# Two interleaved context lanes, doubled weight buffers and six gather landings in a fused transformer kernel

## The reference, cut to what matters

```python
for l in range(2):                                 # first_block, h is 256 x 1024
    ...                                            # attention, w_o, layer norm
    ffn = peer_ffn(h, peer_wq[l], ...)             # 8 heads x 16 experts for each token:
    #   sc = q . sub_keys; top-k twice -> eidx (256 tokens x 128 rows), g = softmax
    #   a = gelu(u[eidx] . h);  ffn = sum over 128 of (g * a) * v[eidx]
    h = layer_norm(ALPHA * h + ffn, ln2_g[l], ln2_b[l])
# second_block
sh1, sc1, g1, sh2, sc2, g2 = split(silu(c) @ w_mod + b_mod, 6)      # modulation
hc = rmsnorm(ctx) * (1 + cm[1]) + cm[0]
sf_c = state_features(hc, ...)                     # Rk, Rv, Gk, Gv, gates (conv for Gk, Gv)
init = recurrent_mixers(sf_c, None, None, zeros)   # retention and gated delta rule states,
#   forward and backward, two chunks of 128 tokens each; depends on ctx alone, not on x
...                                                # the same for x with init, then 64 experts
```

## Time and profile before

| | |
|---|---|
| median of 3 runs | 3200.03 us (3195.45 to 3200.51) |
| the profiled execution | 3195.45 us, span 3193.5 us |
| PE busy | 2481.0 us (78%) |
| DVE busy | 1622.7 us (51%) |
| ACT, POOL busy | 836.7, 824.5 us (26% each) |
| moved by DMA | 885.92 MB, mean 277 GB/s |

### The profile page before, as it was taken

The page is one execution under the profiler, slowest core; times in us unless marked ns, Lnnn a source line. Parts: engine busy times, 40 slices in busy tenths (PEclk is TensorE's granted clock), DMA queues, the critical chain, the costliest instruction groups (busy, mean ns, idle before and its releaser), DMA issues.

```text
span 3193.5 us, 29065 instructions
## 1 busy us (share of the span) xinstructions
PE 2481.0 (78%) x9500; PEld 1316.5 (41%) x9500; DVE 1622.7 (51%) x3307; ACT 836.7 (26%) x2262; POOL 824.5 (26%) x717
## 2 busy tenths in 40 slices
PE   6688888897899868998877877768777667676673
PEld 3665334353455466633322222546553433222221
DVE  4535536879877653664758544264523422111112
ACT  1212333443444131233333333322110111011110
POOL 1001323354465100233344433012000013122221
PEclk9689999999999968999999999889888779888896
DMA  6026978898999702699999999310113199999992
GB/s 258 1 80 264 367 294 337 356 374 326 400 382 391 282 23 80 271 422 422 422 421 417 421 421 386 132 40 27 53 53 148 40 381 400 394 382 389 381 379 80
DMA packets 128898, 885.92 MB, mean 277 GB/s; under 512 B 23008, under 2 KB 23392, under 8 KB 31584
## 3 DMA queue, kind: packets, MB, share of 16 engines
q0 software_dynamic: 86976, 553.74, 43.2%
q1 hardware_dynamic: 41760, 330.22, 25.6%
HBM read 877.56 MB, written 37.75 MB: 287 GB/s over the span
## 4 chain that ended last, share of the span: by engine, by line
PE 42%; DMA 26%; DVE 20%; ACT 5%; issue 4%; POOL 1%; SPq 1%; DVEq 0%; POOLq 0%; ACTq 0%
PE ps L155 41%; DMA ring<-in_peer_uv,idx_u 10%; DVE ring L1256 6%; DMA ring<-in_w_gu 5%; DVE arena L76 5%; ACT arena L125 3%; DMA ring<-in_w_down 3%; DMA arena<-in_w_gu 2%; PE ps L158 2%; DVE arena L97 2%; DMA ring<-in_w_mod 1%; DMA ring<-in_w_in 1%; SPq L2479 1%; DVE iu L113 1%; POOL small L134 1%
## 5 line engine op out<-in xcount | busy, mean ns | idle before, releaser
L155 PE MATMUL ps<-ring,arena 128*128 128x512 f32 (+3 forms) x3264 | 1270.2, 649 | 308.6 <-ACT arena L125 180.8
L155 PEld LDWEIGHTS ps<-ring,arena 128*128 128x128 f32 (+2 forms) x3264 | 472.6, 180 | 988.6 <-issue 606.5
L1256 DVE CUSTOM_DVE_ANT_0 ring<-ring,h 128x1024 f32<-128x1024 f32 x448 | 566.1, 1264 | 331.5 <-DMA ring<-in_peer_uv,idx_u 294.8
L2297 POOL DMA_INDIRECT ring<-in_peer_uv,idx_u x448 | 489.7, 1093 | 811.3 <-PE ps L155 672.9
L155 PE MATMUL ps<-arena 128*128 128x128 f32 (+7 forms) x2504 | 509.8, 389 | 156.6 <-DVE arena L97 45.9
L125 ACT ACTIVATE arena<-arena 128x1 f32<-128x1 f32 (+4 forms) x1129 | 312.9, 277 | 742.4 <-DVE arena L1256 650.5
L155 PEld LDWEIGHTS ps<-arena 128*128 128x128 f32 (+3 forms) x2504 | 328.8, 199 | 332.1 <-issue 158.9
L155 PE MATMUL ps<-ring,hT 128*128 128x512 f32 (+1 forms) x704 | 325.8, 619 | 44.5 <-DMA ring<-in_w_in 22.6
L76 DVE TENSOR_TENSOR arena<-arena,ps 128x512 f32<-128x512 f32 (+1 forms) x158 | 93.6, 592 | 465.2 <-ACT arena L125 356.5
L125 ACT ACTIVATE arena<-ps 128x512 f32<-128x512 f32 (+4 forms) x180 | 99.0, 550 | 834.6 <-PE ps L155 762.8
L125 ACT ACTIVATE arena<-cst,arena 128x128 f32<-128x128 f32 x512 | 205.5, 401 | 155.6 <-PE ps L155 114.2
(11 more groups left out here) (115 smaller groups left out, 1481.9 us busy)
## 6 DMA issues: line engine op xcount, KB each, us to landing
ring<-in_w_gu SPq DMA_DIRECT2D x98, 1024.0 KB, 29.0
ring<-in_w_down SPq DMA_DIRECT2D x52, 1024.0 KB, 29.1
ring<-in_w_in SPq DMA_DIRECT2D x22, 2048.0 KB, 9.8
arena<-in_w_gu SPq DMA_DIRECT2D x30, 1024.0 KB, 29.5
ring<-in_w_mod SPq DMA_DIRECT2D x12, 2048.0 KB
ring<-in_peer_wq SPq DMA_DIRECT2D x8, 2048.0 KB, 7.9
ring<-in_w_o SPq DMA_DIRECT2D x6, 2048.0 KB, 11.6
arena<-in_w_down SPq DMA_DIRECT2D x12, 1024.0 KB, 25.4
```

The costliest lines, as they stand in the source:

```text
L155: return self.e.matmul(o, lhsT, rhs, start=start, stop=stop, skip_group_check=True)
L1256: v.done(v.e.tensor_tensor_reduce(out=row, in0=row, in1=h[:, n // 128, :], scale=1.0, scalar=0.0, op0=ALU.mult, op1=ALU.add, accum_out=aa[ ...
L2297: g.e.indirect_dma_start(out=landing(n), out_offset=None, in_=d["peer_uv"], in_offset=bass.IndirectOffsetOnAxis(ap=idx_u[:, n:n + 1], axis ...
```

## The change

It does five things.

1. GATHERS goes from 8 to 6. The landings in ring 0 to 3 fall away; gathers 4 and 5 wait for the keys, and gather n is issued when gather n - 6 is used.
2. Background weight blocks alternate between ring 0 to 3 (even) and ring 16 to 19 (odd). SP issues block i when block i - 2 is used; the first waits for wq 3, the second for wq 2.
3. The two directions of the context's states, lanes with storage of their own (in the ring's two places and the arena), run side by side, step by step (together), and take PSUM banks from 4 to 7 and 0, 1 (LATE).
4. Modulation takes one step for each block. With the lanes side by side the background of layer 0 has 80 steps: 6, 14, 17, 5 and 38. They stand at n = 4, 7, ... 127 and 138, 141, ... 249. So the states take the 38 steps from 138 on. Layer 1 has 10 steps at n = 4, 14, ... 94.
5. The first w_in block and the second w_o block of layer 1 wait for the lanes' last use. Block Rk of x goes into ring 0 to 3 after modulation block 10, during layer 1's gathers.

```diff
-GATHERS = 8
-SUMS, OTHERS = ((0, 1), (2, 3)), (4, 5, 6, 7)
+GATHERS = 6
+SUMS, OTHERS, LATE = ((0, 1), (2, 3)), (4, 5, 6, 7), (4, 5, 6, 7, 0, 1)
...
     if l:
-        return 1 if n in range(4, 94, 5) else 0
-    return 1 if n in range(2, 130, 2) or n in range(138, 254, 2) else 0
+        return 1 if n in range(4, 104, 10) else 0
+    return 1 if n in range(4, 130, 3) or n in range(138, 252, 3) else 0
...
-        ctx_tiles = [ar(14720 + 512 * i, 512) for i in range(11)] + [ar(512 * i, 512) for i in (1, 2)]
-        ctx_kd = ar(1536, 512)
+        ctx_tiles = [R(i, 1)[:, 512 * j:512 * j + 512] for i in (0, 1, 2, 3, 16, 17, 18, 19) for j in range(2)]
+        ctx_tiles += [ar(14720 + 512 * i, 512) for i in range(9)] + [ar(19328, 512), ar(19840, 512), ar(0, 512)]
+        ctx_lanes = [(ctx_tiles[0:13], ctx_tiles[26]), (ctx_tiles[13:26], ctx_tiles[27])]
...
-            return R(4 + 2 * i, 2) if i < 5 else ar(6144, 2048) if i == 5 else R(2 * i - 12, 2)
+            return R(4 + 2 * i, 2) if i < 5 else ar(6144, 2048)
...
         def BG(i):
-            return R(16, 4)
+            return R(0 if i % 2 == 0 else 16, 4)
...
                 def lane(dr):
+                    TT, kd = ctx_lanes[dr]
                     for c in ((0, 1) if dr == 0 else (1, 0)):
-                        yield from gdn_chunk(s, dr, c, ctx_tiles, OTHERS)
-                        yield from ret_chunk(s, dr, c, ctx_kd, None, OTHERS)
-
-                return chain(lane(0), lane(1))
+                        yield from gdn_chunk(s, dr, c, TT, LATE)
+                        yield from ret_chunk(s, dr, c, kd, None, LATE)
+
+                return together(lane(0), lane(1))
...
-                return chain(lane(0), lane(1))
+                yield from together(lane(0), lane(1))
+                v.tell(("used", "ctx lanes"))
...
             def modulate(blocks, before):
                 for i in blocks:
-                    block(16, 4, d["w_mod"][i], ("loaded", "w_mod", i),
-                          after=[("used", "w_mod", i - 1) if i > blocks[0] else before])
+                    block(0 if i % 2 == 0 else 16, 4, d["w_mod"][i], ("loaded", "w_mod", i),
+                          after=[("used", "w_mod", i - 2) if i - blocks[0] > 1 else before[i % 2]])
...
-                block(0, 4, d["w_in"][l, 0], ("loaded", "w_in", l, 0), after=last)
+                block(0, 4, d["w_in"][l, 0], ("loaded", "w_in", l, 0), after=[("used", "ctx lanes")] if l else ())
...
-                      after=[("used", "ctx", "Gv")] if l else [("used", "ln0")])
+                      after=[("used", "ctx lanes")] if l else [("used", "ln0")])
...
-                before = ("used", "wq", l, 2)
+                before = [("used", "wq", l, 3), ("used", "wq", l, 2)]
...
-                    ctx_block(0, "Rk", ("used", "w_mod", 3))
-                    ctx_block(1, "Rv", ("used", "ctx", "Rk"))
-                    ctx_block(2, "Gk", ("used", "ctx", "Rv"))
-                    ctx_block(3, "Gv", ("used", "ctx", "Gk"))
+                    ctx_block(0, "Rk", ("used", "w_mod", 2))
+                    ctx_block(1, "Rv", ("used", "w_mod", 3))
+                    ctx_block(2, "Gk", ("used", "ctx", "Rk"))
+                    ctx_block(3, "Gv", ("used", "ctx", "Rv"))
...
+            block(0, 4, d["w_in2"][0], ("loaded", "x", "Rk"), after=[("used", "w_mod", 10)])
             block(16, 4, d["w_in2"][4], ("loaded", "x", "Rq"), after=[("used", "w_mod", 11)])
-            block(0, 4, d["w_in2"][0], ("loaded", "x", "Rk"), after=[("used", "gather", 1, 255)])
-            block(4, 4, d["w_in2"][2], ("loaded", "x", "Gk"), after=[])
+            block(4, 4, d["w_in2"][2], ("loaded", "x", "Gk"), after=[("used", "gather", 1, 255)])
```

More of the change, by code:

```diff
@@ L1527, in lane @@
                 def lane(dr):
+                    TT, kd = ctx_lanes[dr]
                     for c in ((0, 1) if dr == 0 else (1, 0)):
-                        yield from gdn_chunk(s, dr, c, ctx_tiles, gsm[dr])
-                        yield from ret_chunk(s, dr, c, ctx_kd, None, None)
-                return chain(lane(0), lane(1))
+                        yield from gdn_chunk(s, dr, c, TT, gsm[dr])
+                        yield from ret_chunk(s, dr, c, kd, None, None)
+                yield from together(lane(0), lane(1))
+                v.tell(("used", "ctx lanes"))
             def second():
@@ L1972, in peer @@
                     if n == NORM_AT[1]:
-                        squares(2 * l + 2, 0, norm_scratch)
+                        squares(2 * l + 2, 0, ar(0, 1024))
                     if n % 64 == EXP_AT and n < 192:
@@ L1978, in peer @@
                     pass
-                squares(2 * l + 2, 1, norm_scratch)
+                squares(2 * l + 2, 1, ar(0, 1024))
             def modulation(i0, i1):
@@ L2294, in gather @@
                     else:
-                        g.wait_ge(*at("used", "wq", l, i // 2) if i < 4 else at("used", "keys", l) if i < 6 else
-                                  at("used", "wq", l, 3))
+                        g.wait_ge(*at("used", "wq", l, i // 2) if i < 4 else at("used", "keys", l))
                     g.e.indirect_dma_start(
@@ L2383, in lane @@
                     for c in ((0, 1) if dr == 0 else (1, 0)):
-                        yield from gdn_chunk(s, dr, c, ctx_tiles)
+                        yield from gdn_chunk(s, dr, c, ctx_lanes[dr][0])
                         yield
-                return chain(lane(0), lane(1))
+                return together(lane(0), lane(1))
             def second():
@@ L2467, in gpsimd_program @@
                 if l == 0:
-                    peer(l, chain(idle(10), context_rows(), conv_features(ctx_side, ctx_side.conv_blocks, ""), idle(5),
+                    peer(l, chain(idle(6), context_rows(), conv_features(ctx_side, ctx_side.conv_blocks, ""), idle(5),
                                   context_states()))
                 else:
-                    peer(l, idle(18))
+                    peer(l, idle(10))
             second()
@@ L2494, in modulate @@
                 for i in blocks:
-                    block(16, 4, d["w_mod"][i], ("loaded", "w_mod", i),
-                          after=[("used", "w_mod", i - 1) if i > blocks[0] else before])
+                    block(0 if i % 2 == 0 else 16, 4, d["w_mod"][i], ("loaded", "w_mod", i),
+                          after=[("used", "w_mod", i - 2) if i - blocks[0] > 1 else before[i % 2]])
             def ctx_block(i, name, before):
-                block(16, 4, d["w_in2"][i], ("loaded", "ctx", name), after=[before])
+                block(0 if i % 2 == 0 else 16, 4, d["w_in2"][i], ("loaded", "ctx", name), after=[before])
             counts = {}
```

6 lines of the change are left out of this document (1 added, 5 removed).

## The result

The changed kernel takes 3237.26 us (median of 4, 3236.73 to 3237.93) against 3197.82 for the kernel before (4 runs, 3195.45 to 3200.51): ratio 1.0124, 95% interval 1.0106 to 1.0141. It is slower by 1.2%, 39 us. The forecast was 3179, the range ended at 3216. The profiled execution took 3248.51 us, 11 us more than any of the four, so differences of single stages against this trace can be that much too large.

The account below looks back on a forecast made before the run. Layer 1 was taken as bound by bytes, layer 0 by DMA, PE and DVE in turns; -9 - 41 + 16 + 10 + 5 - 2.6 = -21.6 on 3195.45 gave 3174 profiled, 3179 for the median, range 3140 to 3216.

Parts of the forecast that it names:

- (a): Modulation in layer 0, gathers 0 to 20: two weight places and one step per block, gather 20 used at 357; -9 us.
- (b): Context rows and convolution, layer 0 gathers 20 to 138: 25 above the floor of 308, so 333 us for 374; -41.
- (c): States, layer 0 gathers 138 to 255: all four chunks, two lanes side by side, 335 us for 319; +16.
- (d): Six landings instead of eight: steady pace unchanged, 5 us lost in layer 1 and 5 in layer 0's stalls; +10.
- rival of the middle's loss coming back: Layer 0, gathers 20 to 138: block waits only move to the gathers, -18 instead of -41; total +1, 3201; chance 0.15.
- a middle as long as before: Sign that the forecast is wrong: layer 0's gathers 20 to 138 not getting shorter than the 374 us before.
- rival of the state phase: Layer 0 from gather 138: doubled start and PE bind, over 357 us, +60 for +16; total +22, 3222; chance 0.20.
- (e): Layer 1 and after: x's Rk block moved into the gather loop, +5.0 us; Rk's first matmuls shorter, -2.6.
- (f): After layer 0's last dot product: layer 1's first w_in block starts a few us earlier under the layer norm; gains nothing.

Follow-up runs that it names:

- e9_chained_late: The changed kernel with all four state chunks still behind gather 138, but one lane after the other in 76 steps: 3250.85 us, ratio 1.0168.
- e7_starts_spread: The changed kernel with only the state steps' places moved, the first four of each pair of chunks five gathers apart: 3234.76 us, ratio 1.0122.
- e5_seven_landings: The kernel before with seven landings instead of eight: 3194.66 us, ratio 0.9993.
- e1_six_landings: The kernel before with six landings instead of eight and nothing else: 3224.66 us, ratio 1.0096.
- e3_chained: The changed kernel with its states one lane after the other as before, 18 of 76 steps ahead of gather 128: 3219.58 us, ratio 1.0081.
- e2_six_places: The kernel before with six landings and two alternating places for background weight blocks, on the old schedule: 3211.95 us, ratio 1.0059.

## Why the prediction was wrong

The forecast's sign is wrong, and 3237 lies outside the range. The profiled execution took 74.5 us more than the 3174 forecast for it: 8 of it in (a), 37 in (b), 27 in (c), 3 in layer 1 and 5 outside the gathers, less the 5 that (d) had set aside for layer 0. By its steps:

**(a) Modulation, -9.** Held in kind. From the first issue to the use of gather 20 it took 103.9 us before. In the changed kernel's own trace it is 102.7, but e9_chained_late and e7_starts_spread, whose programs are the same up to there, took 96.7 and 96.6, so some 6 of the 11 us by which that execution is long lie here. The kernel before may have been long here as well: e5_seven_landings and e1_six_landings, with the same single place for weights, took 98.7 and 98.8. No block of weights stands in the chain of layer 0 any more.

**(b) The middle, -41: the step that failed first.** Gathers 20 to 138 took 370.2 us, not 333; before 374.2. I built it from the floor of 308 and 25 for long steps, as if what else was lost there would go away with the block waits and the state steps. The parts, one upon another, show what became of it: six landings alone 395.8, with two places 380.0, with one step per modulation block and Rk early 372.7 (e3_chained), with the states moved away 370.2. So the six landings took 22 here, the two places gave 16 back, and the states' going gave nothing that could be told from noise: 18 steps, 12 us of PE's work between e3_chained and the changed kernel, cost nothing where they were. The rival of the middle's loss coming back was right in this part, and its sign, a middle as long as before, is what came. Halving the long steps returned 12 to 15 of the 62 us above the floor; which waits make the rest stays open.

**(c) The states, +16: the other step that failed.** 361.9 us instead of 335, and 356.0 in e7_starts_spread, whose profiled execution lies at its median. Levels took 16.75 us per six gathers (two sixes, 809.98 to 843.51: 33.5) where I had 15.7, over 72 gathers 13 us. The two starts, with the routing, took 51 us more than the pace (55.8 and 55.1 for twelve gathers at 29.8) where I had 12 for each and 16 for the routing, 40 in all. The rival of the state phase (decides over 357, total +22) was close, in its levels and in its starts. But the starts are not a loss that can be had back: taking them apart gained 13 us with some work moved out, spreading them 2.5, and doing without them lost 14. What my sum left out is PE's whole work in the stretch: with 309 us in 335 its share would be 0.92, where the stretch had run at 0.88 to 0.89 before. At 0.88 it takes 351. A fourth chunk was moved out of a stretch that did not shorten, into one that was full; between e3_chained and e9_chained_late that costs 31 us, of which side by side saves 14.

**(d) Six landings, +10: mis-sized, it measured +28.** A +16.6, C +6.9, L1 +7.4. Layer 1 came out near the 5 taken for it. What was sized wrongly is the 5 for the stalls of layer 0, which measured 23. The slack was reckoned rightly in kind. A turn needs 10.2 us and has 2.48 for each landing: seven leave 7.2, just over the longest step of 7.1, and lost nothing; six leave 4.7; five leave 2.2 and lose 121. Halving the steps of 7.1 us gave back 13 at six landings; where the other 10 of layer 0 arise was not found. The rows of five landings show PE idle behind the burst and then at its lower clock, and those of the state stretch the DMA at 0.08.

The pace does not fall: five gathers in flight stream at 2.48 us each, as eight do. By the Trainium skill, DMA: Bandwidth & Descriptors, section Bandwidth, efficiency rises with the bytes of a transfer. No run here changes a transfer's size; that the table's figure for one transfer does not apply to a queue of them is what these rows show.

**(e) Layer 1, +5.0 - 2.6.** L1 grew by 13.0: 7.4 landings, 5 the two places. The early Rk block added nothing (704.2 in e3_chained with it, 704.5 in e2_six_places without), perhaps because it fills holes that six landings leave; that was not tested. The first half block of x took 8.50 us for 9.72, so 1.2 back.

**(f) Nothing**, which holds: from the last dot product of layer 0 to layer 1's first issue 247.1 us after 244.4, and 244.3 to 249.3 in all the others.

In sum, by medians and one edit on another: landings +28, places -13, schedule and the rest up to e3_chained +8 (whose cause was not looked for), states moved late +31, side by side -14, together +41 for the 39 measured. The margins of these differences are some 3 to 6 us each.

## What to carry to other kernels

Before background work is moved, compute what each stretch's engines have to do and what share they reached there before; work that leaves a stretch wins time only if that stretch was bound by it, and work that enters a full one can cost more than its own time (29 us of PE work and 37 of time in C of e7_starts_spread). As a first guess of the number of buffers, compare the longest step on the consumer with buffers times pace, less a lone turn from issue to free. Here eight and seven landings covered it and were equal, six cost 28 us and five 121; the size of the loss did not follow from the overrun. When a change bundles places, order and buffers, run its parts by themselves: here a second place for weights helps, 13 us at six landings, and an earlier load into unused memory is worth 12 us on the old kernel, without giving up a landing.

## What the runs showed of the hardware

From eight landings to five (3317.44) the pace of the undisturbed stream did not move from 2.48 us per 1 MB. And DVE and POOL slow each other. In the changed kernel 489 dot products ran without an elementwise operation of POOL beside them, at 1.22 to 1.29 us; those that ran wholly beside one took 2.05 or more. POOL's operation of 128x512 took 1.27 with DVE idle and 1.9 to 2.1 in the rows below. DVE, then POOL:

```profile
954.72 1.22 DVE L1256 CUSTOM_DVE_ANT_0 ring<-ring,h 128x1024 f32<-128x1024 f32 x1
...
958.30 2.05 DVE L1256 CUSTOM_DVE_ANT_0 ring<-ring,h 128x1024 f32<-128x1024 f32 x1
```

```profile
955.41 3.86 POOL L134 TENSOR_TENSOR ring<-ring,cst 128x512 f32<-128x512 f32 x2
959.41 2.06 POOL L134 TENSOR_TENSOR arena<-arena,cst 128x512 f32<-128x512 f32 x1
```

These rows lie in the second start, where both have work for two lanes; how much of its cost this is was not measured by itself.
